# Prompt attention with keys copied once and exchanged by transfers, and idle products shifted around the turns of the recent weights

## The reference

```python
s_c = jnp.einsum('bqkgd,bckd->bkgqc', qg, kc) * scale        # compressed branch
o_c = jnp.einsum('bkgqc,bckd->bqkgd', masked_softmax(s_c, mask_c), vc)
...
s_s = jnp.einsum('bqkgd,bkqnpd->bkgqnp', qrg, k_sel) * scale # selected branch
o_s = jnp.einsum('bkgqm,bkqmd->bqkgd', p_s, v_sel)
...
s_w = jnp.einsum('bqkgd,blkd->bkgql', qrg, kw) * scale       # window branch
o_w = jnp.einsum('bkgql,blkd->bqkgd', masked_softmax(s_w, mask_w), vw)
...
o = gk[..., 0, :] * o_c + gk[..., 1, :] * o_s + gk[..., 2, :] * o_w
```

## Time and profile before

| | |
|---|---|
| median of 3 runs | 1499.48 us (1499.19, 1499.48, 1502.35) |
| time of the profiled execution | 1502.96 us |
| its span, first to last instruction | 1501.3 us |
| TensorE busy | 1462.6 us, 97% of the span |
| VectorE busy | 865.3 us, 58% |
| ScalarE busy | 420.0 us, 28% |
| GpSimd busy | 364.1 us, 24% |
| mean granted clock of TensorE | 0.995 of full speed |
| data moved | 184.36 MB, 123 GB/s in the mean |

### The profile page before, as it was taken

One profiled execution on the slowest core, in us unless ns is written; L12 is line 12 of the kernel. 1 busy time (PEld: TensorE's weight loads), 2 busy tenths in 40 slices (PEclk: granted clock), 3 DMA queues, 4 the chain that ended last, 5 costly groups with the idle time before them and its releaser, 6 DMA issues. The chain is left out here.

```text
span 1501.3 us, 25957 instructions
## 1 busy us (share of the span) xinstructions
PE 1462.6 (97%) x9827; PEld 1221.8 (81%) x9827; DVE 865.3 (58%) x1907; ACT 420.0 (28%) x1063; POOL 364.1 (24%) x479
## 2 busy tenths in 40 slices
PE   8999999899999999999999999999999999999998
PEld 7877899555557888888888889788888888888888
DVE  2754443888545795654667735661585556776513
ACT  3011343788520443334200001442531111000012
POOL 0000300467640359991230034280000000000000
PEclk9999999999989999999999999999999999999999
DMA  8346571311595444463344320712312222322201
GB/s 275 110 128 142 170 214 50 102 49 51 162 352 132 156 166 162 143 228 130 116 133 132 121 68 34 304 34 89 109 60 82 87 99 71 113 84 84 85 28 58
DMA packets 142894, 184.36 MB, mean 123 GB/s; under 512 B 31298, under 2 KB 101642, under 8 KB 141746
## 3 DMA queue, kind: packets, MB, share of 16 engines
q1 hardware_dynamic: 139634, 174.31, 35.6%
q0 software_dynamic: 3136, 8.39, 1.7%
HBM read 163.42 MB, written 29.69 MB: 129 GB/s over the span
## 5 line engine op out<-in xcount | busy, mean ns | idle before, releaser
L2679 POOL TENSOR_SCALAR att_p<-att_p,att_tot,gates 128x128 f32<-128x128 f32 (+3 forms) x128 | 79.6, 636 | 44.9 <-DVE att_tot L2601 44.3
L305 PE MATMUL psum<-xT,l_w 128*128 128x260 f32 x384 | 85.3, 383 | 2.0 <-PEq L113 1.8
L1010 PE MATMUL psum<-xT,l_w 128*128 128x260 f32 x384 | 85.2, 383 | 1.6 <-PEq L113 1.6
L305 PEld LDWEIGHTS psum<-xT,l_w 128*128 128x128 f32 x384 | 72.8, 190 | 13.5 <-issue 2.4
L1010 PEld LDWEIGHTS psum<-xT,l_w 128*128 128x128 f32 x384 | 72.8, 190 | 12.9 <-issue 1.8
L1026 PE MATMUL psum<-l_up_t,l_w_sums 128*128 128x260 f32 x336 | 78.2, 382 | 0.0
L2205 PE MATMUL psum<-cmp_xt,cmp_w 64*128 64x256 f32 (+1 forms) x640 | 72.2, 362 | 0.3 <-DVE cmp_xt L2126 0.3
L1026 PEld LDWEIGHTS psum<-l_up_t,l_w_sums 128*128 128x128 f32 x336 | 63.8, 190 | 9.8
L2652 ACT ACTIVATE att_p<-att_p,att_low 128x128 f32<-128x128 f32 (+3 forms) x128 | 70.4, 554 | 2.8 <-DVE att_low L2592 2.8
L1289 ACT ACTIVATE l_hidden<-l_tmp 128x260 f32<-128x260 f32 x64 | 26.6, 420 | 144.9 <-DVE l_tmp L1439 144.8
L2592 DVE CUSTOM_DVE_ANT_0 att_p<-psum,causal 128x128 f32<-128x128 f32 (+3 forms) x128 | 55.7, 487 | 18.7 <-PE psum L2427 18.1
(11 more groups left out here) (607 smaller groups left out, 3175.2 us busy)
## 6 DMA issues: line engine op xcount, KB each, us to landing
l_w<-in_mlp_w SPq DMA_DIRECT2D x16, 2048.0 KB, 7.8
l_w<-in_mlp_w SPq DMA_DIRECT2D x32, 1024.0 KB, 5.3
proj_w<-in_nsa_w_in SPq DMA_DIRECT2D x4, 2048.0 KB, 9.9
cmp_raw<-in_cache_kv_cmp SPq DMA_DIRECT2D x24, 256.0 KB, 3.1
xT<-in_cache_kv_cmp SPq DMA_DIRECT2D x24, 256.0 KB, 2.9
sa_more<-in_cache_kv_sel POOLq DMA_DIRECT2D x44, 128.0 KB, 6.2
sa_more<-in_cache_kv_sel SPq DMA_DIRECT2D x34, 128.0 KB, 7.0
hT<-in_cache_kv_cmp SPq DMA_DIRECT2D x16, 256.0 KB, 2.9
```

Of the source, the lines that this page charges most:

```text
L305: mm = nc.tensor.matmul(ps[:, n % 8, 0:HALF], w[s][:, k, m * P:(m + 1) * P], src[:, kk, cols(h)], start=(kk == 0), stop=(kk == last))
L1010: mm = nc.tensor.matmul(ps[:, n % 8, 0:HALF], w[s][:, k, m * P:(m + 1) * P], src[:, kk, cols(h)], start=(kk == 0), stop=(kk == last))
L2679: ve.tensor_scalar(pr[:, n % PR, par, at:at + w], pr[:, n % PR, par, at:at + w], tot[:, n % PR, u, par:par + 1], c.gates[:, i, gate:gate + ...
```

## The change

It has two parts. The first is at the begin of the prompt attention. Each key head is copied out of `psum` fewer times. Of kind 0, heads 0 and 1 are copied to both halves of `kT` as before; of the other three banks both heads go over in one copy of 128 partitions, so that each head stands on one half only. The other halves are filled by transfers from `kT` to `kT` that exchange the halves: two for each of the three banks, six in all, issued by SP ahead of all its other work in the stage. `key_slot` tells in which slot a head is found on which half. TensorE waits for the first pair of transfers before round 2 (`near_swapped`) and for the other four before round 20 (`far_swapped`). ScalarE makes an exponential of one element first. Round 0 is issued ahead of the compressed scores of heads 0 and 1; round 1 behind them; those of heads 2 and 3 stand behind round 1. VectorE masks the compressed scores one round earlier, and ScalarE spreads `vcz` one copy a round.

The second part is in the sample attention: six idle products instead of 12 stand ahead of the turns of the window weights, and ten new ones behind them.

```diff
+    exp_ready = c.sem("att_exp_ready")
+    near_swapped, far_swapped = c.sem("att_k_near_swapped"), c.sem("att_k_far_swapped")
...
+        def key_slot(h, par):
+            return h // 2 * 2 + (h % 2 ^ par)
...
-                                                  kT[rows, kind, hp // 2, 0:w], start=True, stop=True)
+                                                  kT[rows, kind, key_slot(hp // 2, par), 0:w], start=True, stop=True)
...
+                pe.wait_ge(k_kept[0], 3)
+                pe.wait_ge(k_kept[1], 2)
+                scores(0)
                 pe.wait_ge(spread, 2)
                 scores_c(0)
                 scores_c(1)
-                for e in range(2):
-                    pe.wait_ge(k_kept[e], 4)
-                scores(0)
+                pe.wait_ge(k_kept[0], 4)
+                scores(1)
                 scores_c(2)
-                for e in range(2):
-                    pe.wait_ge(k_kept[e], 6)
-                scores(1)
                 scores_c(3)
-                for e in range(2):
-                    pe.wait_ge(k_kept[e], 8)
+                pe.wait_ge(k_kept[1], 3)
                 for n in range(2, NU + LAG_PV + 1):
+                    if n == 2:
+                        pe.wait_ge(near_swapped, 32)
+                    if n == 4 * NR:
+                        pe.wait_ge(far_swapped, 64)
...
-                for n in range(4):
+                dve.wait_ge(k_turned, 1)
+                for half in range(2):
+                    rows = slice(half * HD, (half + 1) * HD)
+                    if half == 1:
+                        dve.wait_ge(k_kept[1], 1)
+                    nc.vector.tensor_copy(kT[rows, 0, 0, :], ps[rows, 0, :]).then_inc(k_kept[0], 1)
+                for n in range(1, 3):
                     kind, a = divmod(n, 2)
                     dve.wait_ge(k_turned, n + 1)
-                    for to in range(2):
-                        nc.vector.tensor_copy(kT[to * HD:(to + 1) * HD, kind, 2 * a, :], ps[0:HD, n, :]).then_inc(k_kept[0], 1)
+                    nc.vector.tensor_copy(kT[:, kind, 2 * a, :], ps[:, n, :]).then_inc(k_kept[0], 1)
...
+                    if n == 0:
+                        mask_c(0)
+                    if n == 1:
+                        mask_c(1)
+                    if n == 2:
+                        mask_c(2)
+                        mask_c(3)
                     if 1 <= n <= NU:
...
-                    if n == 1:
-                        mask_c(0)
-                    if n == 2:
-                        mask_c(1)
-                        mask_c(2)
-                    if n == 3:
-                        mask_c(3)
...
+                for n, kept_by, count in ((2, 0, 4), (1, 0, 3), (3, 1, 3)):
+                    kind, a = divmod(n, 2)
+                    sp.wait_ge(k_kept[kept_by], count)
+                    for to in range(2):
+                        sp.dma_start(kT[to * HD:(to + 1) * HD, kind, 2 * a + 1, :],
+                                     kT[(1 - to) * HD:(2 - to) * HD, kind, 2 * a, :]).then_inc(near_swapped if n == 2 else far_swapped, 16)
                 cache.read_table(sp, "sp")
...
                 pe.wait_ge(p_kept[0], 1)
-                keep_awake(c, 5, 12)
+                keep_awake(c, 5, 6)
                 pe.wait_ge(weighed[1], 1)
                 turn_p(1, s_win, s_win[:, WIN:], 6, 0)
+                keep_awake(c, 5, 10)
                 pe.wait_ge(weighed[2], 1)
```

More of the change, by code:

```diff
@@ L2629, in keep_second @@
                     nc.scalar.copy(dst, src).then_inc(kept[1], 1)
-                for n in range(4):
-                    kind, a = divmod(n, 2)
-                    act.wait_ge(k_kept[0], 2 * (n + 1))
-                    for to in range(2):
-                        nc.scalar.copy(kT[to * HD:(to + 1) * HD, kind, 2 * a + 1, :], ps[HD:P, n, :]).then_inc(k_kept[1], 1)
-                act.wait_ge(cleared, 2)
-                for g in range(GRP):
-                    nc.scalar.copy(vcz[32 * g:32 * g + NCP, :, g // 2, g % 2 * HD:(g % 2 + 1) * HD],
-                                   c.vcp[0:NCP, :].rearrange("p (h d) -> p h d", h=NKV)).then_inc(v_spread, 1)
+                nc.scalar.activation(tot[:, 0, 0, 0:1], c.eps[:], ACT.Exp).then_inc(exp_ready, 1)
+                act.wait_ge(exp_ready, 1)
+                act.wait_ge(k_turned, 1)
+                for to in range(2):
+                    if to == 1:
+                        act.wait_ge(k_kept[0], 1)
+                    nc.scalar.copy(kT[to * HD:(to + 1) * HD, 0, 1, :], ps[(1 - to) * HD:(2 - to) * HD, 0, :]).then_inc(k_kept[1], 1)
+                act.wait_ge(k_turned, 4)
+                nc.scalar.copy(kT[:, 1, 2, :], ps[:, 3, :]).then_inc(k_kept[1], 1)
                 for n in range(NU + LAG_PV + 2):
@@ L2653, in _ @@
                                                      bias=low[:, n % PR, u, par:par + 1], accum_out=tot[:, n % PR, u, par:par + 1]).then_inc(exped, 1)
+                    if n < GRP:
+                        if n == 0:
+                            act.wait_ge(cleared, 2)
+                        nc.scalar.copy(vcz[32 * n:32 * n + NCP, :, n // 2, n % 2 * HD:(n % 2 + 1) * HD],
+                                       c.vcp[0:NCP, :].rearrange("p (h d) -> p h d", h=NKV)).then_inc(v_spread, 1)
                     if n < NU:
```

## The result

| | before | after |
|---|---|---|
| median of 20 runs | 1500.53 us (1499.19 to 1503.47) | 1505.28 us (1498.70 to 1507.34) |
| ratio, after to before | | 1.0024, 95% interval 1.0017 to 1.0030 |
| profiled execution, span | 1502.96 us, 1501.3 us | 1499.19 us, 1497.5 us |
| TensorE busy | 1462.6 us | 1458.6 us |
| mean granted clock in the profile | 0.995 | 0.998 |

A forecast was written before the change was run, and what follows sets the result against it. TensorE, busy 97% of the span, was taken as the bound. Profiled 1502.96 less 3.3 (values) and 0.07 (keys) gave 1499.6 us; from the median, 1499.48 less 0.07, rounded to 1499.3; range 1496.8 to 1503.2.

The forecast's parts named there:

- The sum of the work: Whole kernel: profiled 1502.96 us less 3.3 at the values and 0.07 at the keys, giving 1499.6 us.
- the rival of late transfers: Begin of prompt attention: key transfers or SP's queue late, each us past 276.5 costing one; 4 us give 1503.4; chance 0.05.
- the bound of 290: SP queue: first keys for the samples go out at 290 us at the latest, behind six key transfers; no cost.
- the forecast of 1499.3: Whole kernel: 1499.48 less 0.07 us for the keys, rounded to 1499.3; the as-forecast case was 1498 to 1500.5, chance 0.52.
- the first rival: Sample attention: clock falls in the second half of value products, behind the new wait; price 5.1 us, total 1504.7; chance 0.20.
- a pause of 1.96 us at 277.90: Prompt attention before the change: TensorE pause that left the clock alone, used as evidence against the first rival.
- the pause of 1.89 us before: End of sample attention, ahead of the selected weights' turns: clock fell behind it, costing 4.9 us; forecast to be gone.
- The rule: New wait for values, 2.3 us: transposes don't count as busy, so a pause between products brings no fall; 1499.4 us.
- the pause of 1.65 us ahead of round 0: Begin of prompt attention: TensorE idles 1.65 us because compressed products now stand behind round 0; keys net gain 0.07 us.
- The level before: Kernel before: median 1499.48 us read as an execution without the clock fall, so the change brings almost nothing against it.
- The rival in which the change removes losses of the kernel before: Half of the executions before have the fall, none after; median before nearer 1502, key gain up to 1.7 us; chance 0.15.

## Why the prediction was wrong

*The sum of the work was right at full clock.* Round 0 at 3.58 us behind the turns (forecast 3.61), the pause 1.64 (1.65), round 2 lowered at 14.32 (14.46). Round 4 came at 20.93 for 21.41 forecast: the keys gain 0.54 us and not 0.07, 0.29 of it in one operation of VectorE on the compressed sums (L2550), which took 0.20 us for 0.49. The transfers of keys landed in 2.6 us, so the rival of late transfers has nothing to stand on; SP's first keys for the samples went out at 290.34, a little past the bound of 290, and nobody waited for them. At the values, the pause ahead of the selected turns is gone, the first half takes 7.1 us, the wait is 2.25 us (2.3). The three profiled executions without a fall at these places took 1499.19 to 1499.49 us, where the forecast of 1499.3 stands.

*The step that failed* is the weighing of the first rival, a fall of the clock in the second half, at 0.20. Its mechanism, its place, its price (forecast 5.1 us, measured 4.84) and its condition ("in half of the executions or more") were all right: the fall came in six of ten profiled executions. Against it I set that a pause of 1.96 us at 277.90 had left the clock alone, and that the same products had kept full clock. Both were read from one execution. The runs show that one and the same pause lets the clock fall in some executions and not in others: a wait of 1.85 us did so in the execution of 1503.58 us and not in that of 1507.17, and one of 2.25 us did not. A pause that was harmless once is no evidence that it is safe. I had half of this in hand: I took the pause of 1.89 us before as one that lets the clock fall in some executions only, and did not apply it to the new pause. The median of 1505.28 us lies above the 1504.7 of this rival, in a group of which one execution was profiled: 1499.3 plus the 4.84 us at the values and the 1.65 us of the fall near 283 us make 1505.8, and it took 1505.67. The fall near 283 us was in no rival either.

*The rule.* The Trainium skill (TensorE: Matmul & The Clock Gate, Part 4) says that transposes do not count as busy the way products do. From this I concluded that there would be no fall, since the new pause stands between products. The runs don't bear out that use of it: with products on both sides of the pause the clock fell in six of ten.

*A second failed step, in the keys part.* I forecast the pause of 1.65 us ahead of round 0 and priced it in waiting time alone; what a fall of the clock behind it costs was put at nothing. In three of ten profiles it brought 20 to 24 us of half clock. From the start of the turns to round 5 that is 292.86 - 262.88 = 29.98 us, and 284.43 - 262.66 = 21.77 in the first profile: 8.2 us in the execution of 1507.17 us. No rival had this.

*The level before.* I read 1499.48 as the execution without a fall, and 20 runs gave 1500.53, 1 us more. Seven of those 20 executions are at 1499.2 to 1499.9, seven at 1501.56 to 1503.47, and the median lies in a group of six between them (1500.2 to 1500.9), of which there is no profile. The rival in which the change removes losses of the kernel before (0.15) was right in that the old pause is covered: in ten profiles the clock never fell there. What this saves is lost at the new pause.

## What to carry to other kernels

Ask of every pause that a change makes on a busy TensorE what half the clock would cost behind it, and multiply that by a share of executions, not by yes or no; a pause of under 2 us cost up to 8 us here. Then fill it with work that is due anyway (compressed products, steps that don't need the late transfer) and with idle products only for what is left. Before explaining a median, look at how the single executions group: a first profile that falls into the fastest group shows none of what the median is made of.

## What the runs showed of the hardware

The fall is an event of single executions. The same kernel, with the same pause of 1.64 us ahead of round 0 in every profile and a wait for values of 1.76 to 2.42 us, had between 0 and over 30 us at 1.2 GHz in 262 to 470 us (ten profiles). How long it stays low, with TensorE busy, differs by place and execution: 3.4, 7 or 10 us behind the values' wait, and 20 to 24 us behind the pause ahead of round 0, where TensorE was busy 22.16 of 23.40 us. It came from 0.4 us before the end of the wait for values to 1.7 us behind it, and 1.3 to 2.0 us behind the pause ahead of round 0. The shortest pauses by which it stood were 1.28 us near 944 us (it fell in all 18 profiles with a pause of 1.28 or 1.29 there), 1.64 ahead of round 0 and 1.76 at the values. I had not expected so short ones to do it, nor so long a stay.
